# Attention products put in another order, with four pairs of heads in flight instead of three

## The reference

```python
# 16 query heads, 4 key/value heads, head size 64, blocks of 128 queries
def one(qblk):
    s = jnp.einsum('bkgqd,bksd->bkgqs', qblk, k).astype(jnp.float32) * scale
    p = jax.nn.softmax(s, axis=-1).astype(v.dtype)
    return jnp.einsum('bkgqs,bksd->bkgqd', p, v)
```

## Time and profile before

| | |
|---|---|
| median of three runs | 2520.07 us (2515.96 to 2522.47) |
| profiled execution | 2515.34 us, its span 2513.5 us |
| granted TensorE clock, mean over the span | 0.975 |
| TensorE matmul busy | 2334.3 us, 93% of the span |
| VectorE / ScalarE / GpSimd busy | 1489.6 / 794.1 / 233.1 us |
| chain that ended last | TensorE 81%, VectorE 13%, ScalarE 2%, DMA 1% |

### The profile page before, as it was taken

How to read it: one execution, slowest core, us unless ns; L and a number is a source line. 1 busy time by engine, 2 the same in 40 slices (tenths; PEclk the granted TensorE clock), 3 DMA queues, 4 the chain that set the end, 5 groups by cost and what they waited for, 6 DMA issues and landing times.

```text
span 2513.5 us, 35187 instructions
## 1 busy us (share of the span) xinstructions
PE 2334.3 (93%) x14713; PEld 2026.9 (81%) x14713; DVE 1489.6 (59%) x2210; ACT 794.1 (32%) x1421; POOL 233.1 (9%) x257
## 2 busy tenths in 40 slices
PE   5999899988999898999999999899888999999998
PEld 3767857878888888779999999798555789999997
DVE  4376482357434777667565556788666486555654
ACT  4433332210131116344132223533555352222222
POOL 0022040023101330110000000200000110000002
PEclk9999999999999999999999999999898899999999
DMA  7401205520252011222132212122000022221321
GB/s 294 164 26 55 76 1 197 191 78 1 76 206 96 9 51 59 67 101 87 57 96 76 80 59 84 49 76 68 5 1 1 26 72 72 84 75 60 93 68 42
DMA packets 43852, 193.58 MB, mean 77 GB/s; under 512 B 5008, under 2 KB 5008, under 8 KB 36912
## 3 DMA queue, kind: packets, MB, share of 16 engines
q1 hardware_dynamic: 41472, 178.10, 21.3%
q0 software_dynamic: 2224, 13.24, 1.5%
HBM read 183.72 MB, written 7.60 MB: 76 GB/s over the span
## 4 chain that ended last, share of the span: by engine, by line
PE 81%; DVE 13%; issue 2%; ACT 2%; DMA 1%; SPq 0%; DVEq 0%; ACTq 0%
PE pg L836 29%; PE pg L873 16%; PE pg L631 16%; PE ps L782 3%; PE pg L1031 2%; PE ps L1051 2%; DVE att L1784 2%; PE ps L605 2%; DVE wk L1790 1%; PE pg L1006 1%; PE ps L725 1%; DMA ybuf<-in_wada 1%; PE ps L1006 1%; PE ps L729 1%; DVE tp L1788 1%
## 5 line engine op out<-in xcount | busy, mean ns | idle before, releaser
L836 PE MATMUL pg<-hh,xhi 128*128 128x320 f32 (+2 forms) x1008 | 313.7, 311 | 6.5 <-DVE hl L1604 6.5
L836 PE MATMUL pg<-hl,xhi 128*128 128x320 f32 (+2 forms) x1008 | 310.6, 308 | 0.0
L836 PE MATMUL pg<-hh,xlo 128*128 128x320 f32 (+2 forms) x1008 | 310.4, 308 | 0.0
L1490 DVE TENSOR_TENSOR wlo<-ring,whi 128x1024 fp32r<-128x1024 f32 x129 | 157.0, 1222 | 187.9 <-ACT whi L1091 187.7
L631 PE MATMUL pg<-hh,whi 128*128 128x320 f32 x976 | 239.3, 327 | 22.0 <-DVE hl L1522 9.6
L631 PE MATMUL pg<-hl,whi 128*128 128x320 f32 x976 | 225.4, 313 | 0.0
L631 PE MATMUL pg<-hh,wlo 128*128 128x320 f32 x976 | 224.9, 312 | 0.0
L631 PEld LDWEIGHTS pg<-hh,whi 128*128 128x128 f32 x976 | 165.5, 192 | 61.1 <-issue 50.3
L836 PE MATMUL pg<-hh,whi 128*128 128x320 f32 (+2 forms) x672 | 209.2, 311 | 3.3 <-DVE hl L1604 3.3
L836 PE MATMUL pg<-hh,wlo 128*128 128x320 f32 (+2 forms) x672 | 207.3, 308 | 0.0
L836 PE MATMUL pg<-hl,whi 128*128 128x320 f32 (+2 forms) x672 | 207.2, 308 | 0.0
(11 more groups left out here) (309 smaller groups left out, 4661.7 us busy)
## 6 DMA issues: line engine op xcount, KB each, us to landing
ring<-in_wstream SPq DMA_DIRECT2D x231, 512.0 KB, 3.7
adaring<-in_wada SPq DMA_DIRECT2D x21, 1024.0 KB, 5.0
ybuf<-in_wada SPq DMA_DIRECT2D x21, 1024.0 KB, 5.0
adabig<-in_wada SPq DMA_DIRECT2D x6, 1024.0 KB, 18.7
xk<-in_x SPq DMA_DIRECT2D x1, 2560.0 KB, 11.2
yssd_scratch<-ybuf POOLq DMA_DIRECT2D x2, 1280.0 KB, 6.2
xk<-yssd_scratch POOLq DMA_DIRECT2D x1, 2560.0 KB, 11.0
xk<-in_x_tok POOLq DMA_DIRECT2D x1, 2560.0 KB, 10.2
```

Source lines behind the costliest of these rows:

```text
L836: last = nc.tensor.matmul(out, w[:, k * P:(k + 1) * P], h[:, k, a:b], start=k == 0 and m == 0, stop=k == KT - 1 and m == 2)
L1490: V.tensor_tensor(lo, flat(ring[:, s % RING]), hi.bitcast(F32), ALU.subtract).then_inc(wlo_ready, 1)
```

## The change

TensorE's loop turn p before is S(p+1), T0(p-2), T1(p-2), V(p-3), T2(p-2). After, it is T0(p-2), S(p+1), T1(p-2), V(p-3) for the first three key tiles (Va below), T2(p-2), V(p-3) for the last two key tiles (Vb). On VectorE, rest now stands ahead of evac. The buffers of `pr` go round over four pairs, the fourth being `rt` and `rb`, and exp of pair p waits for the last transposes of pair p-4 instead of p-3.

```diff
--- before.py
+++ after.py
@@ -331,8 +331,8 @@
         cvt = adaring[:, 1792:2048]
         def pr(p, par):
 
-            i = 2 * (p % 3) + par
-            return wk[:, i, 0:NT] if i < 4 else sq[:, i - 4, 0:NT]
+            i = 2 * (p % 4) + par
+            return wk[:, i, 0:NT] if i < 4 else sq[:, i - 4, 0:NT] if i < 6 else (rt, rb)[i - 6]
 
 
         def hg_pair(k):
@@ -1032,7 +1032,7 @@
                                                pr(p, par)[:, j * P:(j + 1) * P], cm[:, IDENT, :])
                 last.then_inc(pt_ready, 1)
 
-            def att_pv(p):
+            def att_pv(p, late):
 
                 hp, b = ATT_PAIRS[p]
                 kv = 2 * hp // (ATTN_HEADS // KV_HEADS)
@@ -1044,7 +1044,7 @@
                     pe.wait_ge(pt_rest, by_dve)
                 if p:
                     pe.wait_ge(ao_done, p)
-                for j in range(n):
+                for j in range(3, n) if late else range(min(n, 3)):
                     for par in range(2):
                         v = tiles[par][j]
                         value = (cvt if v == TT else av[:, v])[:, kv * HD:(kv + 1) * HD]
@@ -1055,15 +1055,18 @@
 
             att_scores(0)
             for p in range(NPAIR + 3):
+                if 2 <= p < NPAIR + 2:
+                    att_turn(p - 2, 0)
                 if p + 1 < NPAIR:
                     att_scores(p + 1)
                 if 2 <= p < NPAIR + 2:
-                    att_turn(p - 2, 0)
                     att_turn(p - 2, 1)
                 if p >= 3:
-                    att_pv(p - 3)
+                    att_pv(p - 3, False)
                 if 2 <= p < NPAIR + 2:
                     att_turn(p - 2, 2)
+                if p >= 3:
+                    att_pv(p - 3, True)
             pe.wait_ge(pe_exp, 2 * NPAIR)
             pe.wait_ge(ao_done, NPAIR)
             stage("aout")
@@ -1440,8 +1443,8 @@
                 n = P if ATT_PAIRS[p][1] == PROMPT_TT else NT
                 if par == 0:
                     act.wait_ge(mx_ready, p + 1)
-                    if p >= 3:
-                        act.wait_ge(pt_ready, att_count(p - 2)[0])
+                    if p >= 4:
+                        act.wait_ge(pt_ready, att_count(p - 3)[0])
                 nc.scalar.activation(pr(p, par)[:, 0:n], scores(p, par), ACT.Exp, scale=HD ** -0.5,
                                      bias=mxs[:, p % 4, 1, par:par + 1],
                                      accum_out=mxs[:, p % 4, 2, par:par + 1]).then_inc(pe_exp, 1)
@@ -2028,10 +2031,10 @@
                     att_prob(p - 1)
                 if p + 1 < NPAIR:
                     att_max(p + 1)
+                if 2 <= p < NPAIR + 2:
+                    att_rest(p - 2)
                 if p >= 3:
                     att_evac(p - 3)
-                if 2 <= p < NPAIR + 2:
-                    att_rest(p - 2)
             dve.wait_ge(kv_out, 32)
             for f in range(KT):
                 dve.wait_ge(asc_ready, f + 1)
```

## The result

The changed kernel takes 2494.16 us (four executions, 2492.95 to 2495.87), the kernel before 2520.28. The ratio is 0.9899, with a 95% interval of 0.9885 to 0.9914: about 26 us less. The forecast was 12.5 us less, in a range from 2499 to 2514.

What follows compares the result with a forecast made beforehand. TensorE, busy for 93% of the span, was taken as the bound. Gains of 11.4 us at full clock, 1 in the last turns and 0.5 in the first, taken as 12.5, gave 2520.1 - 12.5 = 2507.5 us, range 2499 to 2514.

Steps and rivals of the forecast that it cites:

- a sum over one turn: TensorE's attention loop at 2.4 GHz: a full turn was to take 4.63 us, 0.53 less than 5.16.

## What to carry to other kernels

Work out a reordering engine by engine as a sum over one turn; with durations from the trace it came out within 3% for each full turn here. But before trusting the base, look at several executions: where time and granted clock go together, find in the profile the stretches with a low clock, and ask of each what your change may do to it; here one of them was worth some 10 us, the reordering itself 14. Then ask of each stop of TensorE whether harmless work fits into it; and before crediting a change with a gain, compare it with a base whose stops are filled.

## What the hardware showed that I had not expected

- Three useless products of 0.67 us in each full pair make the kernel 10 us faster (2519 to 2509 us), and six transposes do the same; 8 of the 10 are gained in the last turns of attention.
- A copy cut in two, which lengthens every TensorE stop from 0.72 to 0.78 us, makes it 5 us faster: 6 us lost among the scores, 8 won in the tail.
- No stop at a fall in the middle or at the tail was longer than 0.78 us: the clock fell in a sparse piece (before, 5.6 us from the end of a full S to the next full V, TensorE busy for 3.6 of them), not in a pause.
- A change between transposes and half-width values costs 0.15 us at 2.4 GHz.
